# Value, gate and branch projections with the tokens stationary and 512 weight columns moving

## The chip, the cores and the metric

The kernel runs on one core of a Trainium2 chip. The metric is device time in microseconds (us) of one execution, the median of several runs. Engines are named as in the profile: PE is the matrix engine (PEld its weight load), ACT the scalar engine, DVE the vector engine, POOL GpSimd, SP the engine whose queue issues the DMAs.

## What is computed

The program computes a hybrid layer on 256 tokens of width 1024 and then a second block with a mixture of experts. Only the first layer is touched here: one wide projection of the normed tokens `h`, four branches of width 512, and a gated sum of the branches' outputs.

```python
h = rms_norm(x, norm_g)
proj = h @ w_in
(a_u, a_v, a_z, b_q, b_c, ..., d_q, d_k, d_v, d_f, d_z, gates) = jnp.split(proj, points, axis=-1)
# y_a .. y_d: four branches, [tokens, 512] each
ys = jnp.stack([y_a, y_b, y_c, y_d], axis=0)
branch_d = jnp.einsum('nbsw,nwd->bsnd', ys, w_branch)      # 512 -> 1024 for each branch
g = jax.nn.sigmoid(gates.reshape(bsz, s, N_BRANCH, d))      # 4 gates of width 1024
merged = jnp.sum(g * branch_d, axis=2)
return x + merged @ w_out
```

## The kernel before

**Weights and their rounding.** All weights of the first part come in blocks of 128 partitions x 4096 numbers, in the order in which they are used. A block is cut into two halves and four quarters. SP's queue loads a quarter into one of four raw slots, ACT copies it rounded to fp32r into a `w_hi` buffer (L1443), POOL writes the rest of the number into `w_lo` (L2925). There are three buffers for halves (`SPLIT`). ACT may round half h only when the fill that read half h - 3 is complete (`readers`); where in ACT's program that stands is decided by `lead_for`, which puts the rounding ahead of the first evacuation whose fill comes later than that reader.

**Products.** A product of two fp32 matrices is three fp32r matmuls (`matmul3`, L484 to L486): hi x lo, hi x hi, lo x hi. `project_T` keeps 128 weight columns stationary and streams 256 tokens; the result has features on partitions. A block of 512 output columns takes 4 x 8 x 3 = 96 matmuls of 256 columns, and so does a branch block (1024 output columns, 4 contraction chunks). `project_tok` is used for the two value blocks `dv` and `av`: tokens are stationary, but the weight halves are halves of the columns, so that 256 columns move in each matmul too, and both halves of the block are given free by the last fill alone.

**Order of the work.** PE runs a list written out by hand: index block, `bq`, `dq`, `dk`, the values `dv` and `av`, `au`, `az`, `dz`, `bz`, `cb`, `cc`, `cx`, `cz`, with attention pieces in between; then for the branches n in `ORDER` = 0, 3, 2, 1 two gate blocks (fills `g{n}0` to `g{n}3`) and a branch block (`br{n}0` to `br{n}3`). A fill is one PSUM bank of 128 x 512; the projections use banks 0, 1, 2 in turn (`PJ`). ACT evacuates the gate fills with a sigmoid (L1466), DVE multiplies each branch fill with its gate and adds it to `merged` (L2249, L2251), which has features on partitions, as the following product with `w_out` needs it. ACT and DVE run their programs in order too: an instruction that waits holds up all behind it on its engine.

Of the kernel before, what the change touches and what calls it, by code (L numbers as in the profile page):

```python
# [8 lines left out]
D = 1024  # L9
SEQ = 256  # L10
P = 128
# [39 lines left out]
class Fill:  # L51


    def __init__(self, b, n, bank, order):
        self.b, self.n, self.bank, self.order = b, n, bank, order

# [15 lines left out]
def build(nc, A):  # L72
# [3 lines left out]
    with ctx:  # L76
# [91 lines left out]
        PJ, WK = (0, 1, 2), (3, 4, 5, 6, 7)  # L168
        H_BANKS = (7, 1, 6, 3)
# [6 lines left out]
        WO = 26  # L176
        FIN, K0, GF, K1, V0, V1, GF2, WF, Q0, Q1, ZB, GD, WD, WO2 = 28, 29, 30, 31, 32, 33, 34, 35, 36, 37, 38, 40, 42, 44
# [29 lines left out]
        score = [g_(P), g_(SEQ)]  # L207
        lg = {a: [g_(NH * P).rearrange("p (h k) -> p h k", h=NH), g_(NH * SEQ).rearrange("p (h k) -> p h k", h=NH)] for a in "fb"}
# [22 lines left out]
        merged, merged_lo_r = chunked(both(KD * SEQ), KD)  # L231

# [231 lines left out]
        def _(pe):  # L464
# [48 lines left out]
            def project_tok(names, b):  # L513

                fs = [begin(name, PJ, 2 * b + i) for i, name in enumerate(names)]
                readers[2 * b] = fs[1]
                for half in range(2):
                    w = halved(b, half)
                    for t, f in enumerate(fs):
                        for k in range(KD):  # L520
                            last = matmul3(f.bank[:, half * SEQ:(half + 1) * SEQ], [m[:, k, t * P:(t + 1) * P] for m in h1],
                                           [m[:, k * SEQ:(k + 1) * SEQ] for m in w], k == 0, k == KD - 1)
                        if half == 1:
                            end(f, last)
# [185 lines left out]
            for n in ORDER:  # L710
                for half in range(2):
                    project_T([f"g{n}{2 * half + j}" for j in range(2)], GATE[n] + half, h1, SEQ)
                pe.wait_ge(sem(f"y{n}"), 2)
                project_T([f"br{n}{j}" for j in range(4)], WB[n], (y_hi[n], y_lo[n]), SEQ, stride=D, kk=CW)
# [156 lines left out]
            def part_product(f, n, x):  # L871

                w = part_weights(n)
                for k in range(KD):
                    c = slice(k * P, (k + 1) * P)
                    last = matmul3(f.bank[:, n % 2 * SEQ:(n % 2 + 1) * SEQ], [m[:, c] for m in w], [m[:, k, :] for m in x],
                                   k == 0, k == KD - 1)
                last.then_inc(full[f.b] if n % 2 or n == 14 else sem("parts"), 1)

            def first_two(f, n, x_hi, x_lo, hi_at, lo_of, pairs_first):  # L880
# [11 lines left out]
                def lo_products(pair):  # L892
                    pe.wait_ge(sem(lo_of), pair + 1)
                    for j, (w_h, _) in enumerate(both_w):
# [3 lines left out]
                        if pair == 3:  # L898
                            last.then_inc(full[f.b] if j else sem("parts"), 1)
# [1051 lines left out]
        def _(dve):  # L1951
# [286 lines left out]
            for i, n in enumerate(ORDER):  # L2238
                for j in range(4):
                    f = got(f"br{n}{j}")  # L2240
                    dve.wait_ge(sem("gate"), 4 * i + j + 1)
                    m = merged[:, 2 * j:2 * j + 2, :]
# [735 lines left out]
        def _(sp):  # L2978
# [74 lines left out]
            def part_done(n):  # L3053

                if n % 2 == 0 and n < 14:
                    sp.wait_ge(sem("parts"), n // 2 + 1)
# [112 lines left out]

def in_columns(m):  # L3170
# [9 lines left out]
def lay_out(I):  # L3180
# [6 lines left out]
    front += [in_halves(w[n]) for n in "bq dq dk dv av au az dz bz cb cc cx cz".split()]  # L3187
    for n in (0, 3, 2, 1):
        front += parts(w["gates"][:, n * D:(n + 1) * D]) + [in_halves(I["w_branch"][0, n])]
# [51 lines left out]
```

## Time and profile before

| | |
|---|---|
| time, median of 3 runs | 1171.86 us (1171.26 to 1172.09) |
| span of the profiled execution, first to last instruction | 1167.6 us |
| the difference, outside the span | 4.3 us |
| PE busy | 1019.9 us (87%), 8173 matmuls |
| POOL busy | 427.5 us (37%) |
| DVE busy | 506.4 us (43%) |
| chain that ended last, by engine | PE 57%, DMA 27%, DVE 8% |

The span has two parts: up to about 650 us the dense layers, where PE is busy nearly all of the time; after it the experts, where the DMA queues move 428 GB/s and PE waits for weights. Busy time of PE counts an instruction from its start to its modelled end, and these overlap: what a matmul costs in a dense row is the distance from its start to the next one's start, and so the rows below are mostly starts.

### The profile page before, as it was taken

How to read it: one execution, taken by the hardware profiler on the slowest of the kernel's cores; microseconds unless marked ns; L12 is line 12 of the kernel's file. 1: busy time of each engine (PE TensorE's matmuls, PEld its weight loads, DVE VectorE, ACT ScalarE, POOL GpSimd, SP SyncE). 2: the span in 40 equal slices, each digit the busy share in tenths (PEclk: the TensorE clock that was granted, in tenths of full speed). 3: DMA queues.
4: the chain of work that ended last, by engine and by line, in shares of the span. 5: the costliest groups of instructions: out<-in, count | busy, mean ns of one | idle time of the engine just before them, and what ended most of it. 6: DMA issues, size and time to landing. Idle time of an engine off the chain costs nothing.

```text
span 1167.6 us, 20205 instructions
## 1 busy us (share of the span) xinstructions
PE 1019.9 (87%) x8173; PEld 802.9 (69%) x8173; DVE 506.4 (43%) x980; ACT 380.4 (33%) x572; POOL 427.5 (37%) x192
## 2 busy tenths in 40 slices
PE   8999999999999999999999899966767667666685
PEld 6999999999999999797989797423323232332231
DVE  4346965601136887767854543222222222222213
ACT  5554354444447656334343344100000000000002
POOL 6767868888876866143031281000000000000000
PEclk9999999999999999999999899988888888888898
DMA  7644546566656544215220889999999999999995
GB/s 248 219 129 146 178 129 187 175 192 186 183 178 196 165 146 137 59 37 217 93 80 12 326 293 383 388 425 428 429 427 428 429 427 429 428 428 429 428 420 202
DMA packets 43569, 304.75 MB, mean 261 GB/s; under 512 B 5092, under 2 KB 5476, under 8 KB 30952
## 3 DMA queue, kind: packets, MB, share of 16 engines
q1 hardware_dynamic: 43208, 303.21, 69.1%
q8 instruction: 51, 0.84, 0.3%
q10 hardware_dynamic: 288, 0.52, 0.1%
q14 instruction: 22, 0.18, 0.0%
HBM read 302.67 MB, written 1.05 MB: 260 GB/s over the span
## 4 chain that ended last, share of the span: by engine, by line
PE 57%; DMA 27%; DVE 8%; POOL 2%; issue 2%; ACT 2%; SPq 2%; DVEq 0%; ACTq 0%; POOLq 0%
DMA arena<-gate_up 24%; PE bank L484 11%; PE bank L485 11%; PE bank L486 10%; PE bank L1357 6%; PE bank L862 5%; PE bank L1378 3%; POOL rounded L2966 1%; DMA weights<-front 1%; DMA arena<-down 1%; PE bank L826 1%; DVE arena L2091 1%; POOL rounded L2925 1%; SPq L3010 1%; PE bank L1097 1%
## 5 line engine op out<-in xcount | busy, mean ns | idle before, releaser
L2925 POOL TENSOR_TENSOR rounded<-weights,rounded 128x1024 fp32r<-128x1024 f32 x152 | 370.4, 2463 | 156.3 <-ACT rounded L1443 146.9
L484 PE MATMUL bank<-rounded 128*128 128x256 f32 (+2 forms) x776 | 219.2, 282 | 2.2 <-POOL rounded L2925 2.2
L485 PE MATMUL bank<-rounded 128*128 128x256 f32 (+2 forms) x776 | 216.5, 279 | 0.0
L486 PE MATMUL bank<-rounded 128*128 128x256 f32 (+2 forms) x776 | 216.2, 279 | 0.0
L1443 ACT ACTIVATE rounded<-weights 128x1024 fp32r<-128x1024 f32 x146 | 147.4, 1052 | 80.6 <-PE bank L486 47.6
L484 PE MATMUL bank<-rounded,rounded 128*128 128x256 f32 (+3 forms) x552 | 158.3, 287 | 2.1 <-DVEq L2346 0.8
L485 PE MATMUL bank<-rounded,rounded 128*128 128x256 f32 (+3 forms) x552 | 156.2, 283 | 0.0
L486 PE MATMUL bank<-rounded,rounded 128*128 128x256 f32 (+3 forms) x552 | 156.1, 283 | 0.0
L484 PEld LDWEIGHTS bank<-rounded 128*128 128x128 f32 (+1 forms) x776 | 145.6, 188 | 4.3 <-POOL rounded L2925 2.9
L485 PEld LDWEIGHTS bank<-rounded 128*128 128x128 f32 (+1 forms) x776 | 145.5, 187 | 0.7 <-issue 0.6
L486 PEld LDWEIGHTS bank<-rounded 128*128 128x128 f32 (+1 forms) x776 | 145.2, 187 | 0.0
L1357 PE MATMUL bank<-arena 128*32 128x512 f32 x512 | 70.1, 707 | 53.5 <-DMA arena<-gate_up 53.5
L1357 PE MATMUL bank<-weights,arena 128*32 128x512 f32 x512 | 70.2, 710 | 49.9 <-DMA weights<-gate_up 48.9
L484 PEld LDWEIGHTS bank<-rounded,rounded 128*128 128x128 f32 (+1 forms) x552 | 103.2, 187 | 4.4 <-issue 1.7
L485 PEld LDWEIGHTS bank<-rounded,rounded 128*128 128x128 f32 (+1 forms) x552 | 103.3, 187 | 0.1
L486 PEld LDWEIGHTS bank<-rounded,rounded 128*128 128x128 f32 (+1 forms) x552 | 103.1, 187 | 0.1
L2833 DVE TENSOR_TENSOR arena<-arena,bank 128x256 f32<-128x256 f32 x16 | 6.7, 421 | 216.8 <-ACT arena L1902 216.8
L1357 PEld LDWEIGHTS bank<-arena 128*32 128x32 f32 x512 | 17.3, 127 | 100.9 <-DMA arena<-gate_up 53.4
L1357 PEld LDWEIGHTS bank<-weights,arena 128*32 128x32 f32 x512 | 17.9, 128 | 96.7 <-issue 96.7
L1902 ACT ACTIVATE arena<-bank 128x256 f32<-128x256 f32 x16 | 6.1, 384 | 235.7 <-PE bank L1357 235.7
L1390 PE MATMUL bank<-arena 128*128 128x512 f32 x128 | 59.3, 605 | 12.6 <-DVE arena L2838 12.6
L1321 PEld LDWEIGHTS bank<-arena 128*128 128x128 f32 x512 | 59.5, 192 | 8.3 <-issue 8.3
(465 smaller groups left out, 1456.6 us busy)
## 6 DMA issues: line engine op xcount, KB each, us to landing
weights<-front SPq DMA_DIRECT2D x165, 512.0 KB, 4.2
arena<-down SPq DMA_DIRECT2D x31, 2048.0 KB, 22.0
weights<-gate_up SPq DMA_DIRECT2D x28, 2048.0 KB, 34.7
arena<-gate_up SPq DMA_DIRECT2D x28, 2048.0 KB, 33.4
weights<-front SPq DMA_DIRECT2D x4, 2048.0 KB, 8.0
weights<-gate_up SPq DMA_DIRECT2D x8, 768.0 KB, 12.5
arena<-gate_up SPq DMA_DIRECT2D x4, 1536.0 KB, 33.7
weights<-gate_up SPq DMA_DIRECT2D x4, 512.0 KB, 7.3
```

Of the source, the lines that this page charges most:

```text
L484: nc.tensor.matmul(out, a[0], b[1], start=start, stop=False)
L485: nc.tensor.matmul(out, a[0], b[0], start=False, stop=False)
L486: return nc.tensor.matmul(out, a[1], b[0], start=False, stop=stop)
L826: last = nc.tensor.matmul(f.bank[0:SUMS, 0:n], row_of[:, SUMS - 1 - c:2 * SUMS - 1 - c], squares[:, h, 0:n], start=h == 0, stop=h == HEADS ...
L862: last = nc.tensor.matmul(f.bank[:, j * n:(j + 1) * n], w[:, c:c + P], x[:, k, :], start=k == 0, stop=k == KD - 1)
L1097: last = nc.tensor.matmul(o, new_v[l.n][:, i, :], qk[:, l.s + i, :], start=not has_state, stop=True)
L1321: last = nc.tensor.matmul(o, m_tok[:, t, k * P:(k + 1) * P], pick_m[:, t, :], start=t == 0, stop=t == TT - 1)
L1357: last = nc.tensor.matmul(banks[3][j * CAP:(j + 1) * CAP, :], xg[:, k, j * CAP:(j + 1) * CAP], gate_up[u][j][:, k * 2 * FE:(k + 1) * 2 * F ...
L1378: last = nc.tensor.matmul(banks[5 + half][j * CAP:(j + 1) * CAP, :], hid_T[:, i, j * CAP:(j + 1) * CAP], down[u][j // 2][:, c:c + 512], st ...
L1390: nc.tensor.matmul(banks[b][:, :], pick_T[:, i % 2 * P:(i % 2 + 1) * P], yb[:, i // 2 * 512:(i // 2 + 1) * 512], start=True, stop=True).th ...
L1443: nc.scalar.activation(w_hi[h % SPLIT][:, quarter(q)], raw[q % RAW], ACT.Copy).then_inc(sem("w_hi"), 1)
L2925: nc.gpsimd.tensor_tensor(lo, raw[q % RAW], hi.bitcast(f32), ALU.subtract).then_inc(sem("w_lo"), 1)
```

## The change

The two value blocks, the six gate blocks of the first three branches and those three branch blocks now have the tokens stationary (128 tokens of `h`, or of a branch's output) and 512 weight columns moving, so that one matmul does what two did: 48 matmuls of 512 columns in place of 96 of 256, in 11 blocks. Their weights are laid out by contraction rows (`in_rows`): a half holds 4 of the 8 contraction chunks and all 512 columns. Both token tiles are open at once; each is filled by the first half and completed by the second. At the end of the first half PE counts up a semaphore of its own, `weights_read`, and ACT may round over that half from then on. The fills use banks 0 to 3 (`TK`).

The gates and products of the first three branches now have tokens on partitions and are added up in `merged_tok`. The fourth branch stays as it was, with features on partitions. Between its two gate blocks PE turns `merged_tok` round with 16 transposes of 128 x 128 into four banks (`mt0` to `mt3`), ACT copies the four banks into `merged`, and DVE waits for these copies before the fourth branch's first product.

```diff
+            def tok_products(f, w, x, ks, t, first, stop):
+                for i, k in enumerate(ks):
+                    last = matmul3(f.bank[:, :], [m[:, k, t * P:(t + 1) * P] for m in x], [m[:, i * W1:(i + 1) * W1] for m in w],
+                                   first and i == 0, stop and i == len(ks) - 1)
+                return last
+            def project_tok(names, b, pool=PJ):
+                fs, half_k = [], KD // 2
                 for half in range(2):
                     w = halved(b, half)
+                    for t, name in enumerate(names):
+                        if half == 0:
+                            fs.append(begin(name, pool, 2 * b + 1))
+                        last = tok_products(fs[t], w, h1, range(half * half_k, (half + 1) * half_k), t, half == 0, half == 1)
                         if half == 1:
+                            end(fs[t], last)
+                    if half == 0:
+                        last.then_inc(sem("weights_read"), 1)
+                readers[2 * b] = Read(IN_ROWS.index(b) + 1, fs[0].order - 0.5)
+            def branch_tok(n):
+                for half in range(2):
+                    w = halved(WB[n], half)
+                    for t in range(TT):
+                        f = begin(f"br{n}{2 * half + t}", TK, 2 * WB[n] + half)
+                        end(f, tok_products(f, w, (y_hi[n], y_lo[n]), range(CW), t, True, True))
...
-            for n in ORDER:
+            for n in ORDER[:3]:
                 for half in range(2):
-                    project_T([f"g{n}{2 * half + j}" for j in range(2)], GATE[n] + half, h1, SEQ)
+                    project_tok([f"g{n}{2 * half + t}" for t in range(TT)], GATE[n] + half, TK)
                 pe.wait_ge(sem(f"y{n}"), 2)
-                project_T([f"br{n}{j}" for j in range(4)], WB[n], (y_hi[n], y_lo[n]), SEQ, stride=D, kk=CW)
+                branch_tok(n)
+            n = ORDER[3]
+            project_T([f"g{n}{j}" for j in range(2)], GATE[n], h1, SEQ)
+            pe.wait_ge(sem("merged"), 4 * 3)
+            for i in range(4):
+                f = begin(f"mt{i}", TK)
...
+                        last = nc.tensor.transpose(f.bank[:, j * SEQ + t * P:j * SEQ + (t + 1) * P], rows[:, k % 4 * P:(k % 4 + 1) * P], ident)
+                end(f, last)
+            project_T([f"g{n}{2 + j}" for j in range(2)], GATE[n] + 1, h1, SEQ)
+            pe.wait_ge(sem(f"y{n}"), 2)
+            project_T([f"br{n}{j}" for j in range(4)], WB[n], (y_hi[n], y_lo[n]), SEQ, stride=D, kk=CW)
...
                         before = readers[h - SPLIT]
-                        act.wait_ge(full[before.b], before.n + 1)
+                        if isinstance(before, Read):
+                            act.wait_ge(sem("weights_read"), before.value)
+                        else:
+                            act.wait_ge(full[before.b], before.n + 1)
...
+                    if i == 3 and j == 2:
+                        for m in range(4):
+                            f = got(f"mt{m}")
+                            link(nc.scalar.activation(merged[:, 2 * m:2 * m + 2, :], two(f.bank), ACT.Copy))
+                            act.sem_inc(free[f.b], 1)
                     evacuate(f"g{n}{j}", gates[:, 2 * j:2 * j + 2, :], "gate", func=ACT.Sigmoid)
```

The order on PE between the fourth branch's two gate blocks; the names give the bank written, the stationary and the moving operand. Before:

```order
L485 MATMUL bank1<-rounded_20112_2048,rounded_8192_2048 128x256
L486 MATMUL bank1<-rounded_20112_2048,rounded_14336_2048 128x256
L484 MATMUL bank2<-rounded_22160_2048,rounded_4096_2048 128x256 [waits bank2_free,w_lo]
L485 MATMUL bank2<-rounded_20112_2048,rounded_4096_2048 128x256
L486 MATMUL bank2<-rounded_20112_2048,rounded_10240_2048 128x256
```

Now, at the same place:

```order
L497 MATMUL bank1<-rounded_20112_2048,rounded_14336_2048 128x256
L752 MATMUL bank0<-arena 128x128 [waits bank0_free,merged]
L752 MATMUL bank0<-arena 128x128 x3
L752 MATMUL bank1<-arena 128x128 [waits bank1_free]
L752 MATMUL bank1<-arena 128x128 x3
L752 MATMUL bank2<-arena 128x128 [waits bank2_free]
L752 MATMUL bank2<-arena 128x128 x3
L752 MATMUL bank3<-arena 128x128 [waits bank3_free]
L752 MATMUL bank3<-arena 128x128 x3
L495 MATMUL bank2<-rounded_22160_2048,rounded_4096_2048 128x256 [waits bank2_free,w_lo]
```

The fill `g12` goes into bank 2 in both; there the third of the four transposed fills now stands ahead of it.

The order on ACT at that place (L1466 and L1511 are the sigmoid of a gate fill, L1443 and L1488 the rounding of a quarter). Before:

```order
L1466 ACTIVATE arena<-bank1 128x512 [waits bank1_full]
L1443 ACTIVATE rounded_8192_2048<-weights 128x1024 [waits act_chain,slot0_in,bank1_full,merged]
L1443 ACTIVATE rounded_8192_2048<-weights 128x1024 [waits slot1_in]
L1466 ACTIVATE arena<-bank2 128x512 [waits bank2_full]
L1443 ACTIVATE rounded_4096_2048<-weights 128x1024 [waits act_chain,slot2_in,bank2_full,merged]
```

Now:

```order
L1511 ACTIVATE arena<-bank1 128x512 [waits bank1_full]
L1488 ACTIVATE rounded_8192_2048<-weights 128x1024 [waits act_chain,slot0_in,bank1_full,merged]
L1488 ACTIVATE rounded_8192_2048<-weights 128x1024 [waits slot1_in]
L1622 ACTIVATE arena<-bank0 128x512 [waits bank0_full]
L1622 ACTIVATE arena<-bank1 128x512 [waits act_chain,bank1_full]
L1622 ACTIVATE arena<-bank2 128x512 [waits act_chain,bank2_full]
L1622 ACTIVATE arena<-bank3 128x512 [waits act_chain,bank3_full]
L1511 ACTIVATE arena<-bank2 128x512 [waits act_chain,bank2_full]
```

The four copies stand behind the sigmoid of `g11` and behind the rounding of two quarters.

The order on ACT during the block `av`, between the two parts of a softmax's exponentials (L1544, now L1589). Before:

```order
L1544 ACTIVATE arena<-arena 128x256 x3
L1443 ACTIVATE rounded_6144_2048<-weights 128x1024 [waits slot2_in,bank1_full]
L1443 ACTIVATE rounded_6144_2048<-weights 128x1024 [waits slot3_in]
L1443 ACTIVATE rounded_8192_2048<-weights 128x1024 [waits slot0_in,bank1_full]
L1443 ACTIVATE rounded_8192_2048<-weights 128x1024 [waits slot1_in]
```

Now:

```order
L1488 ACTIVATE rounded_6144_2048<-weights 128x1024 [waits slot2_in,weights_read]
L1488 ACTIVATE rounded_6144_2048<-weights 128x1024 [waits slot3_in]
L1589 ACTIVATE arena<-arena 128x256 [waits soft_max]
L1589 ACTIVATE arena<-arena 128x256 x3
L1488 ACTIVATE rounded_8192_2048<-weights 128x1024 [waits slot0_in,bank1_full]
L1488 ACTIVATE rounded_8192_2048<-weights 128x1024 [waits slot1_in]
```

The rounding of the first of the two halves no longer waits for the end of the block (`bank1_full`) but for `weights_read`, and has moved ahead of the second part of the exponentials.

## Rows read from the trace of the kernel before

**Rows 1.** The page, part 4: the chain that ended last, by engine.

```profile
PE 57%; DMA 27%; DVE 8%; POOL 2%; issue 2%; ACT 2%; SPq 2%; DVEq 0%; ACTq 0%; POOLq 0%
```

**Rows 2.** Stretches: us, then busy us of each engine (instructions), clock, DMA share, GB/s.

```profile
204.80:340.50 135.70, 135.70 (x1154) 135.70 (x1153) 37.57 (x39) 60.02 (x68) 114.52 (x48) 1.00 0.62 184
```

**Rows 3.** Timeline of PE (start, us, operation): matmuls of 256 columns.

```profile
89.81 0.28 PE L485 MATMUL bank<-rounded 128*128 128x256 f32 x1
102.73 0.28 PE L485 MATMUL bank<-rounded 128*128 128x256 f32 x1
...
204.83 0.28 PE L485 MATMUL bank<-rounded 128*128 128x256 f32 x1
337.69 0.28 PE L485 MATMUL bank<-rounded,rounded 128*128 128x256 f32 x1
```

**Rows 4.** Timeline of PE: fp32r matmuls of 132 and of 272 columns.

```profile
15.50 0.22 PE L484 MATMUL bank<-rounded 128*128 128x132 f32 x1
15.56 0.28 PE L485 MATMUL bank<-rounded 128*128 128x132 f32 x1
...
384.82 0.29 PE L484 MATMUL bank<-rounded,rounded 128*32 128x272 f32 x1 [0.19 <-DVEq L2315]
387.70 0.29 PE L486 MATMUL bank<-rounded,rounded 128*32 128x272 f32 x1
...
407.58 0.29 PE L485 MATMUL bank<-rounded,rounded 128*128 128x272 f32 x1
431.29 0.29 PE L484 MATMUL bank<-rounded,rounded 128*128 128x272 f32 x1
```

**Rows 5.** Timeline of PE: plain f32 matmuls of 256 columns, and what follows.

```profile
559.65 3.62 PE L862 MATMUL bank<-arena,weights 128*128 128x256 f32 x16
563.10 1.05 PE L993 MATMUL bank<-arena 128*128 128x128 f32 x8
```

**Rows 6.** Timeline of PE: transposes of 128 x 128, and what follows.

```profile
533.68 2.79 PE L849 MATMUL bank<-arena 128*128 128x128 f32 x24
536.40 1.92 PE L956 MATMUL bank<-arena 16*16 16x128 f32 x16
```

**Rows 7.** Timeline of ACT and PE between the fourth branch's two gate blocks.

```profile
317.55 0.28 PE L485 MATMUL bank<-rounded 128*128 128x256 f32 x1
317.98 0.60 ACT L1466 ACTIVATE arena<-bank 128x512 f32<-128x512 f32 x1 [2.48 <-PE bank L486]
318.86 2.01 ACT L1443 ACTIVATE rounded<-weights 128x1024 fp32r<-128x1024 f32 x2 [0.28 <-ACT arena L1466]
```

**Rows 8.** Timeline of PE and ACT around PE's three waits from `av` to `cc`.

```profile
97.72 3.91 ACT L1443 ACTIVATE rounded<-weights 128x1024 fp32r<-128x1024 f32 x4 [6.72 <-PE bank L486]
102.84 0.28 PE L486 MATMUL bank<-rounded 128*128 128x256 f32 x1
104.11 0.38 PE L484 MATMUL bank<-rounded 128*128 128x256 f32 x1 [0.99 <-POOL rounded L2925]
140.91 1.13 PE L637 MATMUL bank<-arena 128*128 128x256 f32 x4 [0.73 <-DVEq L2180]
165.84 0.39 PE L484 MATMUL bank<-rounded 128*128 128x256 f32 x1 [1.19 <-POOL rounded L2925]
```

**Rows 9.** The chain that ended last, in order of time, 60 to 360 us.

```profile
97.79 0.71 DVE arena L2153
...
133.01 0.70 DVE rounded L1985
...
135.22 2.79 DVE rounded L1985
...
160.59 5.21 POOL rounded L2925 x2
```

**Rows 10.** Stretches around two falls of the granted clock; columns as in rows 2.

```profile
653.50:657.70 4.20, 0.10 (x1) 0.00 (x0) 4.10 (x7) 1.64 (x3) 0.50 (x1) 0.86 1.03 400
656.50:663.40 6.90, 5.65 (x26) 5.68 (x27) 5.86 (x9) 4.57 (x7) 5.53 (x3) 0.51 1.03 435
79.50:83.10 3.60, 3.13 (x18) 2.37 (x16) 2.04 (x4) 3.12 (x4) 1.39 (x1) 1.00 0.00 0
83.10:86.50 3.40, 3.40 (x10) 2.72 (x9) 2.07 (x3) 3.37 (x7) 3.40 (x3) 0.50 0.43 108
```

More of the change, by code:

```diff
@@ L55, in __init__ @@
         self.b, self.n, self.bank, self.order = b, n, bank, order
+class Read:
+    def __init__(self, value, order):
+        self.value, self.order = value, order
 class Lane:
@@ L168, in build @@
         PJ, WK = (0, 1, 2), (3, 4, 5, 6, 7)
+        TK = (0, 1, 2, 3)
         H_BANKS = (7, 1, 6, 3)
@@ L176, in build @@
         WO = 26
+        IN_ROWS = [DV, AV] + [GATE[n] + c for n in ORDER[:3] for c in range(2)]
         FIN, K0, GF, K1, V0, V1, GF2, WF, Q0, Q1, ZB, GD, WD, WO2 = 28, 29, 30, 31, 32, 33, 34, 35, 36, 37, 38, 40, 42, 44
@@ L207, in build @@
         score = [g_(P), g_(SEQ)]
+        lg_at = top[0]
         lg = {a: [g_(NH * P).rearrange("p (h k) -> p h k", h=NH), g_(NH * SEQ).rearrange("p (h k) -> p h k", h=NH)] for a in "fb"}
@@ L231, in build @@
         merged, merged_lo_r = chunked(both(KD * SEQ), KD)
+        merged_tok = arena[:, lg_at + 2 * W1:lg_at + 2 * W1 + TT * D].rearrange("p (k t) -> p k t", k=KD)
         top[0] = layer_base
@@ L877, in part_product @@
                                    k == 0, k == KD - 1)
-                last.then_inc(full[f.b] if n % 2 or n == 14 else sem("parts"), 1)
+                last.then_inc(full[f.b] if n % 2 or n == 14 else sem("weights_read"), 1)
             def first_two(f, n, x_hi, x_lo, hi_at, lo_of, pairs_first):
@@ L898, in lo_products @@
                         if pair == 3:
-                            last.then_inc(full[f.b] if j else sem("parts"), 1)
+                            last.then_inc(full[f.b] if j else sem("weights_read"), 1)
                 for pair in range(pairs_first): hi_products(pair)
@@ L2240, in _ @@
                     f = got(f"br{n}{j}")
-                    dve.wait_ge(sem("gate"), 4 * i + j + 1)
-                    m = merged[:, 2 * j:2 * j + 2, :]
+                    dve.wait_ge(sem("gate"), 4 * i + (j if i < 3 else max(j, 2)) + 1)
+                    m = (merged_tok if i < 3 else merged)[:, 2 * j:2 * j + 2, :]
                     g = gates[:, 2 * j:2 * j + 2, :]
@@ L3055, in part_done @@
                 if n % 2 == 0 and n < 14:
-                    sp.wait_ge(sem("parts"), n // 2 + 1)
+                    sp.wait_ge(sem("weights_read"), len(IN_ROWS) + n // 2 + 1)
                 else:
@@ L3167, in in_halves, with in_rows @@
     return m.reshape(-1, P, 2, m.shape[1] // 2).transpose(1, 2, 0, 3).reshape(P, BLOCK)
+def in_rows(m):
+    return m.reshape(2, -1, P, m.shape[1]).transpose(2, 0, 1, 3).reshape(P, BLOCK)
 def in_columns(m):
@@ L3186, in lay_out @@
     front = [in_halves(np.concatenate([w["bc"], w["wi"], w["ki"], w["df"], pad, w["qi"]], 1))]
-    front += [in_halves(w[n]) for n in "bq dq dk dv av au az dz bz cb cc cx cz".split()]
+    front += [(in_rows if n in ("dv", "av") else in_halves)(w[n]) for n in "bq dq dk dv av au az dz bz cb cc cx cz".split()]
     for n in (0, 3, 2, 1):
-        front += parts(w["gates"][:, n * D:(n + 1) * D]) + [in_halves(I["w_branch"][0, n])]
+        gate = w["gates"][:, n * D:(n + 1) * D]
+        front += (parts(gate) if n == 1 else [in_rows(gate[:, :W1]), in_rows(gate[:, W1:])]) + [in_halves(I["w_branch"][0, n])]
     front += parts(I["w_out"][0])
```

12 lines of the change are left out of this document (4 added, 8 removed).

## The prediction, made before the changed kernel was run

> **What bounds the kernel now.** First the chain that ended last: PE holds 57% of it, DVE only 8% [rows 1]. Then the stretch that the change rewrites: from 204.8 to 340.5 us PE does not stop, and the 1154 matmuls that touch it (12 blocks of 96, and two cut by the edges) take 135.7 us; POOL, the next busiest, has 114.5 us to do there [rows 2]. So in the gate and branch blocks a nanosecond saved or added on PE is one on the clock. Around the value blocks it is different: there the chain in order of time leaves PE at 97.79 us, when `av` is complete, and runs over DVE (with few breaks) to 160 us, then over POOL to PE's next wait [rows 9]. What PE saves between these points it may wait out later.
>
> The third view is the pace of PE, start to start. From 204.83 to 337.69 us there are 1128 steps: 117.8 ns for one matmul of 256 columns. From 89.81 to 102.73 us there are 114 steps: 113.3 ns, with the same shapes and the same granted clock [rows 3]. So there are two paces; the change's nine gate and branch blocks ran at the slow one, `av` at the fast one.
>
> **Streaming: 1056 matmuls of 256 columns become 528 of 512.** The streamed columns are the same, 256 columns at 2.4 GHz are 106.7 ns, and what a wider matmul can save is the surcharge: 11.1 ns at the slow pace, 6.7 at the fast one. The question is whether that is paid for each instruction or for each column, and no fp32r matmul of 512 columns is in the trace. Rows nearest to it:
> - 272 columns take 126.1 ns (188 steps from 407.58 to 431.29 us) and 125.2 ns with only 32 stationary columns to load (23 steps from 384.82) [rows 4]. A surcharge of 11.1 ns each would give 113.3 + 11.1 = 124.4; the same price for each column (117.8 / 256 = 0.460 ns) gives 125.2.
> - 132 columns take about 0.06 us [rows 4]. 55 + 11.1 would be 66 ns; 132 x 0.460 is 61.
> - 16 plain f32 matmuls of 256 columns take 3.45 us, 215.6 ns each [rows 5]; at two cycles a column that is 213.3 ns and 2.3 ns of surcharge, though just as many weights are loaded.
>
> The load of the stationary columns therefore isn't the surcharge (32 columns cost what 128 cost), and three lengths of fp32r lie on one price for each column better than on one for each instruction. Bounds for 512 columns: 215.6 ns (rows 5, only the small surcharge left) and 235.6 ns (twice the present matmul, nothing saved). I take 234, near the upper end, since rows 4 are the same data type and rows 5 are not: the price for each column, less part of the 2.3 ns that rows 5 show for each instruction.
> Gates and branches: 432 x (235.6 - 234) = 0.7 us saved. `dv` the same, 48 x 1.6 = 0.1 us if it ran at the slow pace. `av`: 48 x (226.7 - 234), a loss of 0.35 us. Together 0.4 us saved; by the bounds between 0.5 us lost (48 x (235.6 - 226.7) on `av`) and 432 x 20 + 48 x 20 + 48 x 11 = 10.1 us saved.
>
> Of this step the Trainium skill ("TensorE: Matmul & The Clock Gate", section "Back-to-back issue gap") says that a warm matmul of N columns is followed by the next one after N/2.4 + 2.5 ns, which is 215.8 ns for 512 columns and 109.2 for 256. The trace agrees for plain f32 (215.6 ns for 512 cycles, rows 5) and disagrees for fp32r at 256 columns (117.8 and 113.3, rows 3). By the page the sum below would end near 1166.9 us.
>
> **Sixteen transposes and what stands behind them.** A transpose of 128 x 128 costs 113 ns (24 in 2.72 us) [rows 6]: 16 are 1.8 us. The copies by ACT cost more, because of where they stand. As the order shows, ACT first evacuates `g11`, then rounds two quarters, then copies `mt0` to `mt3`; and PE's next fill, `g12`, goes into bank 2, which the third copy sets free. From the trace of that place: ACT starts on `g11` at 317.98 us (0.60 us), starts the rounding at 318.86 and takes 2.01 us, to 320.87 [rows 7]. Three copies of a bank at 0.60 us each, with the 0.28 us between two linked ACT instructions that rows 7 show: 3 x 0.60 + 2 x 0.28 = 2.36, to 323.2, and 0.28 more until PE sees it: 323.5. Before, PE started `g12` at 317.55 [rows 7]. The delay is 6.0 us, of which PE transposes for 1.8, waits 0.7 us or so for bank 1 (`g11` must be out of it before `mt1`) and some 3.3 us for bank 2. ACT and POOL get ahead in this time, but PE was not waiting for them here, so nothing of it comes back; DVE and the fourth branch are all behind `g12`. Bounds: 1.8 us (the transposes alone, all copies hidden) and 6.0 plus a fall of the clock. I take 6.0, since each link is a row and ACT runs in order.
> The clock: after a wait of PE of 4.2 us it was at 1.2 GHz (0.51) for 6.9 us, and after 3.6 us with 18 small matmuls at 1.2 GHz (0.50) for 3.4 us [rows 10]. The new place is like the second. If the clock falls, 3.4 us at half speed cost 1.7 us more. I give that 4 in 10 and leave it out of the middle.
>
> **The read signal.** In `av` ACT rounded nothing from the end of the exponentials until 97.72 us, when the block was complete; that wait was 6.72 us. Four quarters in a row then came late, and PE stood from 102.95 to 104.11 us in `au` [rows 8]: 1.2 us. With `weights_read` the first two quarters are rounded when half of `av` is read, about 5.4 us earlier, and POOL has them done before PE asks. This stop goes. What is late next: PE waits for DVE at 140.91 us already now (0.73) and for POOL at 165.84 (1.19) [rows 8], both ends of the DVE chain that begins with `av`. If that chain stays as it is, all of the 1.2 us is waited out there. But POOL's two quarters leave the stretch in which they hold DVE back (the same DVE instruction takes 0.70 us in one place of the chain and 2.79 in another, rows 9), so that the chain should shorten too. Bounds: nothing, and the three stops together, 3.1 us. I take 1.0. The wait moved ahead of ACT's second part of exponentials delays these by some 5 us; DVE asks for them only after `av`, so it costs nothing; if DVE asked sooner, at most the same 5 us would be at stake.
> In the gate blocks the signal changes nothing: PE never waited for weights there [rows 2].
>
> **Edits that cost nothing.** DVE's products and sums have the same shapes in `merged_tok`. The fourth bank only eases the turns. SP and POOL issue the same transfers and subtractions in the same order.
>
> **The sum.** 1171.9 + 6.0 - 1.0 - 0.4 = 1176.5 us. It is made on one execution with a span of 1167.6 us; the 4.3 us up to the median of the runs lie outside the span and stay. After the gates the chain runs through PE to the experts' loads, which PE's progress releases, so the shift should reach the end whole.
>
> **Rivals.**
> 1. The surcharge is paid for each instruction, and 512 columns cost 215.6 to 224.4 ns (213.3 and 2.3 or 11.1). For: the fast pace exceeds 106.7 ns by the same 16 cycles in every step, as a fixed cost would. Against: rows 4. With 221 ns: 432 x 14.6 + 48 x 14.6 + 48 x 5.7 = 7.3 us saved, 1171.9 + 6.0 - 1.0 - 7.3 = 1169.6 us, faster; with 215.6 ns 1166.8, with 224.4 ns 1171.5. It decides in favour of the change from about 221 ns down. The skill's gap rule is this rival's lower end.
> 2. The price is by the column, but the wide matmuls run at the fast pace, 0.443 ns a column or 226 ns with a little off. For: `av`, tokens stationary, ran at it. Against: `project_T` blocks ran at both paces, so the form didn't decide it. 432 x 9.6 + 48 x 9.6 = 4.6 us saved: 1172.3 us, no difference.
> 3. The change doesn't do what it says at the read signal: PE's stop in `au` goes, and all of it returns at 140.91 and 165.84 us. Then the forecast ends at 1177.5 us; a fall of the clock as well gives 1179.2.
>
> **Chances and range.** Forecast with rival 3 (1175 to 1179): 0.53. Rival 1: 0.30. Rival 2: 0.17. A measurement of this kernel can tell 0.2%, 2.3 us, from no change: faster is below 1169.5, slower above 1174.2. Faster: two thirds of rival 1, 0.20. Same: the rest of rival 1, most of rival 2 and a little of the forecast, 0.26. Slower: 0.54. The range must reach into rival 1, down to 217 to 218 ns for 512 columns, 1168.0; at the top it takes in the fall of the clock, 1179.0.
>
> **What would show it.** Right: starts of the 512-column matmuls 233 to 236 ns apart in the gate blocks; PE stopped for 3 us or more ahead of `g12`, released by ACT's copy line, 6 us from the last matmul of `g11` to the first of `g12`; no stop in `au`, a longer one at the logits of `b`. Wrong: starts 216 to 222 ns apart (rival 1), or 226 (rival 2); ACT's copies done before the rounding, so that PE goes on after 2 us.

## The result, and the profile after

| | before | after |
|---|---|---|
| time, median of 19 runs each | 1171.41 us (1167.12 to 1175.79) | 1175.0 us (1169.97 to 1178.52) |
| ratio, 95% interval | | 1.0027 (1.0015 to 1.0038) |
| span of the profiled execution | 1167.6 us | 1173.3 us |
| PE busy, matmuls | 1019.9 us, 8173 | 1026.5 us, 7661 |

The changed kernel is slower by 0.27%, 3.6 us where 4.6 were forecast. For each of its runs the span is known too: it is 1.7 to 1.8 us below the time, and 1.7 to 2.0 in 43 of the 45 runs of the kernel before that list it. By that the profiled execution of before, with its span of 1167.6 us, was one of about 1169.3 us, 2 us better than the median, and the 4.3 us that were put outside the span were in part that difference. One run of e3 (below), 1678.6 us at a mean granted clock of 0.554, is left out of its figures.

Page, part 4, the chain that ended last, by engine (answers [rows 1]):

```profile
PE 60%; DMA 26%; DVE 5%; ACT 2%; POOL 2%; issue 2%; SPq 2%; ACTq 0%; DVEq 0%; POOLq 0%
```

Three points of the chain, some 35 us, have passed from DVE to PE. From 97.8 to 129 us the chain of before ran over DVE; now DVE is done sooner there and waits for PE, as its row at 125.27 us shows below.

**The wide matmuls.** Timeline of PE, the second 512-column matmul of the gates and the last of the third branch (answers [rows 3]), and the stretch between them, with the columns of [rows 2]:

```profile
204.77 0.40 PE L496 MATMUL bank<-rounded 128*128 128x512 f32 x1
...
305.10 0.40 PE L497 MATMUL bank<-rounded,rounded 128*128 128x512 f32 x1
```

```profile
204.80:305.10 100.30, 100.30 (x432) 80.81 (x430) 35.52 (x29) 43.70 (x49) 87.12 (x37) 1.00 0.62 184
```

430 steps in 100.33 us are 233.3 ns each; 234 was taken. 432 of them are 0.97 us less than 864 at 117.8. In `av`, which had run at 113.3 ns, the 48 wide ones cost 0.32 us more (233.3 against 226.7).

**The place of the transposes.** Timeline of PE and ACT between the fourth branch's two gate blocks (answers [rows 7]; L1511 is the sigmoid, L1488 the rounding, L1622 the copies):

```profile
316.52 0.28 PE L497 MATMUL bank<-rounded 128*128 128x256 f32 x1
316.64 0.60 PE L752 MATMUL bank<-arena 128*128 128x128 f32 x4
316.84 0.60 ACT L1511 ACTIVATE arena<-bank 128x512 f32<-128x512 f32 x1 [2.77 <-PE bank L497]
317.54 1.53 PE L752 MATMUL bank<-arena 128*128 128x128 f32 x12 [0.29 <-ACTq L1512]
317.71 2.00 ACT L1488 ACTIVATE rounded<-weights 128x1024 fp32r<-128x1024 f32 x2 [0.27 <-ACT arena L1511]
319.62 2.72 ACT L1622 ACTIVATE arena<-bank 128x512 f32<-128x512 f32 x4
321.81 0.55 PE L495 MATMUL bank<-rounded 128*128 128x256 f32 x1 [2.75 <-ACTq L1623]
322.16 0.41 PE L496 MATMUL bank<-rounded 128*128 128x256 f32 x1
```

From the last matmul of `g11` to the first of `g12` PE needs 321.81 - 316.52 = 5.29 us, where one step of 0.12 us stood: 5.2 us lost, 6.0 forecast. The reader should see the order on ACT: sigmoid, two roundings, and only then the four copies, the third of which ends the 2.75 us wait. And the matmuls that follow stand 0.21 us apart instead of 0.118: the clock fell to 0.50, 1.2 GHz. The same columns as above, for the stretch of the stop and the one behind it:

```profile
316.60:321.80 5.20, 2.18 (x18) 1.71 (x17) 0.00 (x0) 4.33 (x7) 4.29 (x3) 0.95 0.64 197
321.80:324.60 2.80, 2.79 (x13) 2.80 (x14) 0.00 (x0) 0.54 (x1) 1.71 (x1) 0.50 0.79 199
```

**The read signal.** ACT and PE from `av` to `cc` (answers [rows 8]):

```profile
92.16 2.01 ACT L1488 ACTIVATE rounded<-weights 128x1024 fp32r<-128x1024 f32 x2 [5.17 <-PE bank L497]
97.76 2.01 ACT L1488 ACTIVATE rounded<-weights 128x1024 fp32r<-128x1024 f32 x2 [1.62 <-PE bank L497]
...
139.67 1.13 PE L665 MATMUL bank<-arena 128*128 128x256 f32 x4 [0.49 <-DVEq L2230]
164.84 0.38 PE L495 MATMUL bank<-rounded 128*128 128x256 f32 x1 [1.43 <-POOL rounded L2975]
```

Two quarters are rounded at 92.16 us instead of behind 97.72, PE's stop in `au` is gone, and the later waits are 0.49 and 1.43 us (0.73 and 1.19 before). PE starts the logits at 139.67 instead of 140.91: 1.2 us are kept. The next two rows, one of before and one of after, show why the chain of DVE shortened with it: the same four instructions, first beside twelve subtractions of POOL in a row, then for the most part in a pause of POOL (115.44 to 118.03 us). The third row, of after, is DVE's next one: it waits for PE.

```profile
118.67 10.20 DVE L2091 SCALAR_TENSOR_TENSOR arena<-arena 128x256 f32<-128x256 f32 x4
```

```profile
116.64 4.07 DVE L2141 SCALAR_TENSOR_TENSOR arena<-arena 128x256 f32<-128x256 f32 x4
125.27 0.70 DVE L2239 TENSOR_TENSOR bank<-bank,arena 128x512 f32<-128x512 f32 x1 [4.55 <-PE bank L712]
```

The Trainium skill ("SBUF — State Buffer", section "SBUF: two separate sides") says that VectorE and GpSimd share a port pair that one of them holds for a whole instruction. The trace agrees: 10.20 against 4.07 us, of which the three instructions in POOL's pause took 0.48 us each and the fourth, beside POOL, 2.52.

**What the clock did elsewhere.** Summed over stretches of 1 us up to 700 us (busy time of PE times one minus the granted clock), the falls of the clock cost 6.2 us in three places before and 9.7 us in six places after. One of these is the fall behind the stop (1.4 us); two more (1.7 us each, at 457 and 468 us) lie in code that the change doesn't touch. Between 698 and 785 us, where the experts' weights are awaited, the lag of the changed kernel shrinks from 8.6 to 6.3 us. That is no waiting out of the lag: e1 (below), level with the kernel before at 698 us, gains 1.8 us in the same stretch, and the second profile of before (e10) loses 0.5. SP issues twelve transfers of experts' weights there in 7.1 us in the changed kernel and 7.9 in e1, and in 8.7 in either profile of before; why is not shown.

### The profile page after: what moved, and what is told of

The parts are those of the page before. It is cut to its first block, busy times and chain, and to the rows that moved or that the text cites. A ratio compares the mean times of both kernels' runs of the same rounds, so it can differ in the third digit from the quotient of the medians.

```text
span 1173.3 us, 19188 instructions
## 1 busy us (share of the span) xinstructions
PE 1026.5 (87%) x7661; PEld 785.7 (67%) x7661; DVE 502.9 (43%) x980; ACT 382.3 (33%) x576; POOL 425.1 (36%) x192
## 4 chain that ended last, share of the span: by engine, by line
PE 60%; DMA 26%; DVE 5%; ACT 2%; POOL 2%; issue 2%; SPq 2%; ACTq 0%; DVEq 0%; POOLq 0%
DMA arena<-gate_up 24%; PE bank L495 12%; PE bank L497 11%; PE bank L496 11%; PE bank L1399 6%; PE bank L904 5%; PE bank L1420 3%; DMA weights<-front 1%; POOL rounded L3016 1%; PE bank L868 1%; POOL rounded L2975 1%; DMA arena<-down 1%; SPq L3060 1%; PE bank L1139 1%; PE bank L1118 1%
## 5 line engine op out<-in xcount | busy, mean ns | idle before, releaser
L495 PE MATMUL bank<-rounded 128*128 128x256 f32 (+3 forms) x648 | 199.1, 307 | 4.2 <-ACTq L1623 2.7
L497 PE MATMUL bank<-rounded 128*128 128x256 f32 (+3 forms) x648 | 196.2, 303 | 0.0
L496 PE MATMUL bank<-rounded 128*128 128x256 f32 (+3 forms) x648 | 196.2, 303 | 0.0
L1488 ACT ACTIVATE rounded<-weights 128x1024 fp32r<-128x1024 f32 x146 | 147.1, 1052 | 98.5 <-PE bank L497 78.3
L495 PE MATMUL bank<-rounded,rounded 128*128 128x256 f32 (+4 forms) x504 | 151.4, 300 | 2.7 <-POOL rounded L3016 1.0
L497 PE MATMUL bank<-rounded,rounded 128*128 128x256 f32 (+4 forms) x504 | 149.1, 296 | 0.0
L496 PE MATMUL bank<-rounded,rounded 128*128 128x256 f32 (+4 forms) x504 | 149.0, 296 | 0.0
L495 PEld LDWEIGHTS bank<-rounded 128*128 128x128 f32 (+1 forms) x648 | 122.0, 188 | 12.1 <-POOL rounded L2975 5.1
L496 PEld LDWEIGHTS bank<-rounded 128*128 128x128 f32 (+1 forms) x648 | 121.9, 188 | 6.1 <-issue 0.2
L497 PEld LDWEIGHTS bank<-rounded 128*128 128x128 f32 (+1 forms) x648 | 122.0, 188 | 5.8
L495 PEld LDWEIGHTS bank<-rounded,rounded 128*128 128x128 f32 (+1 forms) x504 | 95.0, 188 | 7.2 <-issue 1.8
L496 PEld LDWEIGHTS bank<-rounded,rounded 128*128 128x128 f32 (+1 forms) x504 | 95.0, 189 | 2.3
L497 PEld LDWEIGHTS bank<-rounded,rounded 128*128 128x128 f32 (+1 forms) x504 | 95.0, 188 | 2.3
L1399 PEld LDWEIGHTS bank<-arena 128*32 128x32 f32 x512 | 17.7, 129 | 97.8 <-DMA arena<-gate_up 51.8
```

The costliest lines, as they stand in the source:

```text
L495: nc.tensor.matmul(out, a[0], b[1], start=start, stop=False)
L496: nc.tensor.matmul(out, a[0], b[0], start=False, stop=False)
L497: return nc.tensor.matmul(out, a[1], b[0], start=False, stop=stop)
L1399: last = nc.tensor.matmul(banks[3][j * CAP:(j + 1) * CAP, :], xg[:, k, j * CAP:(j + 1) * CAP], gate_up[u][j][:, k * 2 * FE:(k + 1) * 2 * F ...
L1488: nc.scalar.activation(w_hi[h % SPLIT][:, quarter(q)], raw[q % RAW], ACT.Copy).then_inc(sem("w_hi"), 1)
```

## The experiments

**Take the stop away.** First another four banks for the transposed fills, then DVE as well in place of ACT for the copies:

```diff
-                f = begin(f"mt{i}", TK)
+                f = begin(f"mt{i}", (4, 5, 6, 7))
```

```diff
-                        for m in range(4):
-                            f = got(f"mt{m}")
-                            link(nc.scalar.activation(merged[:, 2 * m:2 * m + 2, :], two(f.bank), ACT.Copy))
-                            act.sem_inc(free[f.b], 1)
...
+                if i == 3:
+                    for m in range(4):
+                        evacuate(f"mt{m}", merged[:, 2 * m:2 * m + 2, :])
```

> The changed kernel, but the four transposed fills go into banks 4 to 7 instead of 0 to 3, so that the fill g12 no longer needs the bank that ACT's third copy sets free; ACT's copies stay where they are. Theory 'bank wait': in the changed kernel PE went from the last matmul of g11 (316.52 us) to the first of g12 (321.81) in 5.3 us and then ran 12 matmuls at the low clock (1.2 us lost). Here that step takes 1.9 to 2.2 us (16 transposes at 113 ns), the clock stays at 1.00, and 4.3 to 4.6 us come back: about 1170.5 us, ratio to the kernel before 0.9985 to 1.0000. Rival 'ACT is the limit': the copies still stand ahead of the sigmoid of g12 and of the next rounding, PE stops later at a bank of g13 or of the branch, and the time stays within 1 us of the changed kernel's 1175.0. Rival 'the transposes lower the clock': the step is short but the half clock comes all the same, 1171.7 us.

> As e1_far_banks, and the four copies are made by DVE, which was busy 0.00 us between 316.5 and 322 us, instead of ACT. Theory 'bank wait': with the banks out of the way the copies are hidden anyway, so this lies within 0.5 us of e1_far_banks in the trace up to the end of the fourth branch. Rival 'ACT is the limit': at least 1 us faster than e1_far_banks there, since 2.7 us of copies leave ACT's program.

Measured: 1168.04 us, ratio to before 0.9971 (0.9960 to 0.9982), and 1168.01 us, 0.9969 (0.9955 to 0.9983). Timeline of PE and ACT at the place in e1, and the clock of the two stretches behind it:

```profile
314.76 1.91 PE L752 MATMUL bank<-arena 128*128 128x128 f32 x16
314.96 0.60 ACT L1511 ACTIVATE arena<-bank 128x512 f32<-128x512 f32 x1 [2.77 <-PE bank L497]
315.83 2.01 ACT L1488 ACTIVATE rounded<-weights 128x1024 fp32r<-128x1024 f32 x2 [0.27 <-ACT arena L1511]
316.43 0.36 PE L495 MATMUL bank<-rounded 128*128 128x256 f32 x1
317.74 2.73 ACT L1622 ACTIVATE arena<-bank 128x512 f32<-128x512 f32 x4
```

```profile
316.40:319.20 2.80, 2.80 (x27) 2.80 (x26) 0.00 (x0) 2.56 (x5) 2.23 (x1) 1.00 0.72 200
319.20:321.60 2.40, 2.40 (x23) 2.40 (x23) 0.00 (x0) 1.16 (x2) 2.40 (x2) 1.00 0.50 125
```

ACT copies at the same point of its program as in the changed kernel, but PE is back on `g12` 1.67 us after the first transpose, and the clock stays at 1.00. So the bank was the wait, the clock did not fall where PE did not stop, and ACT was not the limit: in e2, without the copies, the trace is that of e1 within 0.1 us up to 480 us. The gain was larger than expected, 7 us against 4.6. Of it 3.5 us are the stop, 1.4 to 3.1 the clock behind it, and 0.85 us a surprise: in e1 and e2 the matmuls from 316.6 to 338 us ran at 113.3 ns instead of 117.8 (191 steps); in e7, with the same banks, they ran at 117.8. This version beats both kernels. The terms account for 0.3 us of the 3.4 under the kernel before (1.7 for the transposes, less 1.0 at the read signal and 1.0 for the wide matmuls of gates and branches); the 1.8 us at the experts are the largest other piece that the traces show.

**One half of the change each.** e3 is the kernel before with `dv` and `av` changed and nothing else (`IN_ROWS = [DV, AV]`); e6 is e1 with these two blocks as before (`IN_ROWS` without them).

> The kernel before with the two value blocks dv and av alone changed (512 columns moving, halves by rows, read signal); gates and branches as before, no transposes. Theory: PE reaches its wait for POOL at cc (before: first matmul after it at 165.84) about 1.2 us earlier, as in the changed kernel; the blocks cx and cz decide how much of it is left at the first gate: if they run at 117.8 ns as in the changed kernel 0.2 us, if at 113.3 as in the kernel before 1.1 us; the gates and branches then take as long as before. Time 1170.3 to 1171.4, ratio 0.9990 to 1.0000. Rival 'the loss is in the value blocks': ratio 1.002 or more.

> The other half of e3: gates and branches as in e1_far_banks (512 columns moving, read signal, transposed fills in banks 4 to 7), the two value blocks as in the kernel before. Theory: up to the first gate it is the kernel before, with its stop in au; then the nine blocks give back 1.0 us (432 times 235.6 - 233.3) and the transposes cost 1.8: about 1 us over the kernel before, ratio 0.9995 to 1.0015. Rival 'the gates carry the gain': e1_far_banks was 3.5 us under the kernel before and e3_values_only 2.6, so that this part would bring 0.9 us of its own: ratio 0.9985 to 0.9995.

Measured: e3 1168.4 us in the median and 1169.5 in the mean of eleven runs, 0.9981 (0.9967 to 0.9996); e6 1169.57 us, 0.9988 (0.9973 to 1.0003). The product, 0.9969, is what e1 and e2 have: within these intervals the halves add up. e3 gained 2.2 us, more than the 0.2 to 1.1 expected, though its interval reaches down to 0.5; its trace is 1.2 us ahead of before at 141 us, as in the changed kernel. e6 doesn't separate its two theories. Its trace agrees with the first up to `g12` (317.75 us against 317.55, with 0.4 us gained by chance in `dv`); after that the fast pace as in e1 gives 0.85 us back, which neither theory had.

**Take the read signal away**, in all eight blocks:

```diff
-                readers[2 * b] = Read(IN_ROWS.index(b) + 1, fs[0].order - 0.5)
+                readers[2 * b] = fs[1]
```

> The changed kernel without the read signal: ACT waits for the end of the block again before it rounds over a first half, in all eight blocks. Theory 'the chain shortens': PE's stop of some 1.2 us in au returns (near 103 us), the DVE chain behind it stretches again, PE starts the logits of b near 141 us instead of 139.67, and the first gate comes about 1.2 us later than in the changed kernel: ratio to the kernel before 1.003 to 1.004. Rival 'absorbed': the stop in au returns, but the waits at the logits of b and at cc shrink by as much, and from 166 us on the trace is that of the changed kernel: ratio 1.0027.

Measured: 1184.04 us, 1.0102 (1.0082 to 1.0121): 9 us above the changed kernel, not 1.2. Waits of PE in the gates and branches, two of them in the timeline, and ACT ahead of the first:

```profile
PE bank L495 <- POOL rounded L2975: 7.6, 6, 1.3
```

```profile
218.14 3.90 ACT L1488 ACTIVATE rounded<-weights 128x1024 fp32r<-128x1024 f32 x4 [0.25 <-ACT arena L1511]
...
224.06 0.50 PE L495 MATMUL bank<-rounded 128*128 128x512 f32 x1 [1.21 <-POOL rounded L2975]
236.74 0.50 PE L495 MATMUL bank<-rounded,rounded 128*128 128x512 f32 x1 [1.20 <-POOL rounded L2975]
```

The stop in `au` returns (0.78 us), and the wait at the logits grows to 3.00 us, so "absorbed" is wrong. But most of the loss lies where nothing was expected: six stops of 1.2 to 1.3 us, ahead of the second half of the second gate block and of the branch block, for each of the three branches. In the kernel before, the first half of a gate block was free when the first of two fills was complete, in the middle of the block. With halves by contraction rows no fill completes before the end; the half that takes that buffer (three halves later) is rounded late, four quarters come due at once, and POOL needs some 2.4 us for each. The signal gives back what the new layout of the weights takes away.

**The falls of the clock: place or chance?** Both kernels once more.

> The changed kernel once more, for a second profile. Theory 'the falls of the clock come by chance except where PE stops': the fall behind g12 (322 to 325 us) comes again, with the 2.7 us wait for ACT ahead of it; the falls at 82 and 457 to 472 us need not come at the same places. Rival 'every fall belongs to its place': all six falls at the same places as in the first profile.

> The kernel before once more, for a second profile of it. Theory 'falls by chance': the fall at 83 to 87 us need not come again, nor the fast pace in av, cx and cz; the span differs from 1167.6 us by the count of falls times 1.7 us and some tenths of pace. Rival 'every fall and every pace belongs to its place': the same falls, the same blocks at 113.3 ns.

The same two stretches in the first and the second profile of the kernel before (the clock is the number before the DMA share):

```profile
83.00:87.00 4.00, 4.00 (x14) 3.21 (x14) 2.29 (x5) 3.97 (x10) 4.00 (x3) 0.57 0.45 126
452.00:456.00 4.00, 4.00 (x35) 4.00 (x36) 3.30 (x8) 3.62 (x7) 2.32 (x1) 1.00 0.56 156
```

```profile
83.00:87.00 4.00, 4.00 (x29) 3.79 (x29) 3.50 (x5) 3.97 (x10) 4.00 (x3) 1.00 0.44 125
452.00:456.00 4.00, 4.00 (x24) 4.00 (x23) 2.98 (x7) 3.79 (x6) 1.37 (x1) 0.57 0.77 222
```

One fall is gone and another has come, with the same program (0.57 over a stretch of 4 us is a fall to 0.50 for most of it). `cx` and `cz`, at 113.3 ns in the first profile, ran at 117.8 in the second. In the changed kernel's second profile the fall behind `g12` came again, and cost 3.1 us; the one at 82 us did not. Over all ten profiles of the layer, the fall behind `g12` is there in the three that have the stop and in none of the seven that don't. That one belongs to its place. So do two that the change doesn't touch, near 11 and at 656 to 677 us, which all ten profiles have; the others come and go, at 1.6 to 1.7 us each. The mean granted clock of all runs is in line with this: the span times one minus that clock is 67.2 us on average in the 19 runs of the changed kernel, 65.9 in 45 of the kernel before, and 64.5 and 65.0 in the 12 each of e1 and e2.

**What does a wide matmul cost?** First in the kernel: e1 with each matmul of 512 columns cut into two of 256.

> e1_far_banks with each 512-column matmul cut into two of 256 with the same stationary block (weights loaded twice): the layout without the wide matmul. Theory 'price per column': the gate and branch blocks of the first three branches run at 117.8 ns a piece, 1.0 us longer than in e1_far_banks from the first gate to the last matmul of the third branch (100.5 us there), or, where they start at the fast pace, at 113.3, which is 2.9 us shorter. Rival 'a price for each instruction': more than 4 us longer in every case.

Timeline of PE, a matmul of the first gate block and the last one before the transposes:

```profile
205.64 0.28 PE L495 MATMUL bank<-rounded 128*128 128x256 f32 x1
...
313.65 0.28 PE L497 MATMUL bank<-rounded 128*128 128x256 f32 x1
```

953 steps in 108.0 us: 113.3 ns. A pair costs 226.7 ns where the wide one costs 233.3, so that the narrow form was 2.9 us shorter over 432 pairs. (One run: 1167.65 us.)

Then by itself, in programs of trains of 48 matmuls, each after a stop of another length. They compute no output.

> Not the layer: a program of matmuls alone (no output is computed, zeros are written), to measure the disputed price by itself. Trains of 48 fp32r matmuls of one width, stationary blocks of 128 columns, each train after a stop of PE of another length. Widths 64 to 512, then 14 trains each of 256 and 512 in turn, then 272 and 384; two trains with only 32 stationary columns, two in plain f32. Theory 'price per column': start to start 0.456 ns a column for all widths of 256 and more, 512 always near 233.3 ns, 384 near 175, and 256 now at 117.8, now at 113.3 ns, decided at a train's start. Rival 'a price for each instruction': 512 near 224, 384 near 171. Rival 'the wide matmuls have a fast pace too': some of the 14 trains of 512 run near 226.7 ns.

> Again matmuls alone (no output is computed, zeros are written), 256 and 512 columns in the patterns of the kernel, since in e5 a matmul of 512 columns took 227 ns and not the 233.3 of the changed kernel. Patterns: alternating operands; the same, added up in one bank; the kernel's three products (hi x lo, hi x hi, lo x hi) written anew and added up; with the roles of the two tensors swapped; one stationary block and one moving block all the time. Theory 'the order of operands sets it': the three products give 233.3 ns for 512 columns and 113.3 or 117.8 for 256 with every other engine idle. Rival 'adding up in PSUM sets it': both added-up patterns give 233.3. Rival 'the other engines' (their reads of the same memory): every pattern stays at 227 here, and at 120 for 256 columns.

> Matmuls alone a third time (zeros are written), now with the buffers of the kernel itself: tokens (h, hi and lo) and weights (the three buffers w_hi and w_lo) at their places, in the order of tok_products with 512 and with 256 columns and in that of project_T. Of the five rounds of nine trains the third and fourth run beside transfers into the raw slots, the fifth beside POOL's subtractions. Theory 'the places of the operands': 512 columns take 233.3 ns in every round, and 256 take 117.8 or 113.3. Rival 'the transfers': 227 in the first two rounds, 233.3 in the third and fourth. Rival 'the compute engines': 227 but in the fifth. If all rounds show 227 and 120, none of the three is the reason, and it stays open.

> Matmuls alone a last time (zeros are written): the weights stay at their place, the tokens are moved through memory, to offsets of 0 to 1680 columns (modulo 2048) from the weights; 1680 is where the kernel's h lies, 0 is the layout of e5 and e9; both come twice. For each offset one train of 512 columns and one of 256 with the tokens stationary, two of 256 with the weights stationary. Theory 'the distance of the operands sets the pace': 0 gives 227 and 120 ns, 1680 gives 233.3 and 113.3 or 117.8, in both places of the list, and the offsets between group with the one or the other. Rival 'it was something else in the layout' (the spacing of the hi and lo buffers, the blocks' strides): every offset gives the same.

In e5 none of the theories held whole: inside a train 256 columns took 119.9 ns, 320 took 146.7, 384 took 173.3 and 512 took 227, which is N / 2.4 and 13.3 ns for each instruction (448 took 202.7, 2.7 ns more than that, and 272 took 125.2 to 126.7). The 227 ns are those of the last theory, but all 15 trains had them, and 256 stayed at 120. With 32 stationary columns 256 took 117.8 and 512 took 231.7. e9 has the kernel's order and adds up in PSUM, and stays at 227 and 120. e11 has the kernel's buffers at their places: 512 columns take 233.3 ns in all 15 trains, beside transfers and POOL or not. e12 moves the tokens only. Timeline of PE, trains of 48; the second number is the length of the train. At offset (in columns from the weights, modulo 2048) 1680, then 0, 16 and 64, each time 512 columns and then 256 with the tokens stationary:

```profile
45.08 11.46 PE L491 MATMUL bank<-rounded,rounded 128*128 128x512 f32 x48 [0.51 <-ACT arena L504]
57.10 5.73 PE L491 MATMUL bank<-rounded,rounded 128*128 128x256 f32 x48 [0.56 <-ACT arena L504]
...
76.61 11.22 PE L491 MATMUL bank<-rounded,rounded 128*128 128x512 f32 x48 [0.69 <-ACT arena L504]
88.55 6.02 PE L491 MATMUL bank<-rounded,rounded 128*128 128x256 f32 x48 [0.73 <-ACT arena L504]
...
108.22 11.46 PE L491 MATMUL bank<-rounded,rounded 128*128 128x512 f32 x48 [0.44 <-ACT arena L504]
120.16 5.73 PE L491 MATMUL bank<-rounded,rounded 128*128 128x256 f32 x48 [0.48 <-ACT arena L504]
...
139.45 11.21 PE L491 MATMUL bank<-rounded,rounded 128*128 128x512 f32 x48 [0.61 <-ACT arena L504]
151.33 6.02 PE L491 MATMUL bank<-rounded,rounded 128*128 128x256 f32 x48 [0.66 <-ACT arena L504]
```

11.46 us are 233.3 ns inside the train, 11.2 are 227; 5.73 are 113.4, 6.02 are 120. The offsets 1680 (twice) and 16 give the first pair, the offsets 0 (twice), 64, 128, 256, 512, 1024, 1536 and 1664, all multiples of 64 columns, the second; both offsets of the first group are 16 above a multiple of 64, and no other was tried. So the place of the tokens in memory sets the price, and it decides which form is cheaper: 233.3 against 2 x 113.4, or 227 against 2 x 120. Whether their distance from the weights counts or their own address is not shown, since the weights stayed at a multiple of 2048. At the kernel's offset one more thing counts, the form: with tokens stationary 11 of 15 trains of 256 ran at 113.4 ns in e11, with weights stationary 2 of 15. With weights stationary in e12 256 took 117.8 ns at 1680 and 16, 120 at the other offsets. What the memory does there is not shown.

One row of the kernel before belongs to this, the third of the group of 132 columns whose first two [rows 4] show:

```profile
15.67 0.28 PE L486 MATMUL bank<-rounded 128*128 128x132 f32 x1
```

The first step of each such group is 60 to 63 ns, the second 110; in a longer row, from 20.1 to 22.5 us, these matmuls stand 110 to 114 ns apart.

## Why the prediction was right, and where not

- **What bounds the kernel.** Held: PE didn't stop in the gates, and what PE lost at `g12` was lost to the stages behind it, as e1 shows from the other side.
- **Streaming, -0.4 us.** The taken price was 234 ns, the measured one 233.3, and the blocks gained 0.8 us together (0.97 in gates and branches, 0.1 in `dv`, less 0.32 in `av`). The reason given for it, a price for each column, is no law: e5 shows the price for each instruction of rival 1, at 227 instead of 215.6 to 224.4 ns, at offsets that the kernel doesn't have. The prediction's rows could not tell that, since their tokens lay at the kernel's own places. One of its three lengths also says less than was taken from it: the 0.06 us of 132 columns are the first step of a group of three (60 to 63 ns each time), and the next step in the same group is 0.11 (15.56 to 15.67 us), as in longer rows of them. Rival 2's fast pace for wide matmuls came in none of 15 trains of e11 and in none of the kernel's profiles; the argument against it, that the form doesn't decide the pace, was too strong, since it shifts the odds.
- **The stop ahead of `g12`, +6.0 us.** The mechanism was the predicted one, link by link; it measured 5.2, and the wait in it 2.75 us where 3 or more were named as the sign. The copies follow one another in 0.71 us, where 0.60 and 0.28 had been added (0.35 us for three), and the rounding ended 0.3 us earlier after the last matmul of `g11`. 16 transposes take 1.67 us (e1) and not 1.8.
- **The clock, left out at 4 in 10.** This is the term that was mis-sized: the fall came in all three profiles with the stop and cost 1.4 to 3.1 us. It belonged in the middle of the sum, and the 1.7 us named for it fit two of the three; in the second profile of the changed kernel (e8) the fall lasted twice as long.
- **The read signal, -1.0 us.** Right in size (PE 1.2 us ahead at the logits, 1.0 behind its wait at `cc`) and in mechanism: POOL's work moved ahead of DVE's, and DVE's chain shortened. Rival 3 fell. The sign that PE's wait at the logits would be longer did not come: it was 0.49 us, not 0.73, and only the one at `cc` grew, by 0.24. Wrong was the sentence that the signal changes nothing in the gate blocks. It was tested against the kernel before, where a fill did what the signal does now; without it the new layout costs 9 us (e4).
- **The sum.** With the clock's 1.4 us it would have been 5.2 + 1.4 - 1.0 - 1.0 = 4.6 us (the first 1.0 is the lead behind `cc`, with the value blocks' 0.1 and 0.32 in it, the second the gates and branches); 3.6 were measured, with an interval of 1.8 to 4.5. That this is again the 4.6 of the forecast is luck: a stop taken 0.8 us too long and a saving taken 0.6 too small made up for the clock that was left out. The pace of blocks that nothing touched accounts for tenths in either direction (`cx` and `cz` 0.85 us), single falls of the clock for 1.7. "The shift should reach the end whole" held up to 698 us (PE 5.4 us late from 338 to 440 us, 8.6 at 698 with two falls more); behind that the profile of after gains 2.3 us, and e1, which had no lag, 1.8, so that it was not the lag that was waited out there. What it was stays open.

## What to carry to other kernels

When a step is inserted on PE, ask which bank the next fill takes and where the instruction that frees it stands in its engine's order: the 16 transposes cost 1.7 us with free banks and 5.2 us with a bank freed by the third copy behind two roundings, and a stop of that kind costs the clock behind it too. When the layout of a shared buffer changes, ask what now tells its reader that a part is free; a signal that looks like an addition may be the replacement of one that the layout removed. And a price for each column or each instruction should be measured at the operands' own addresses before a change is built on it.

## What was not expected of the hardware

- An fp32r matmul of 256 columns took 113.3, 117.8 or 120 ns and one of 512 took 227 or 233.3, at the full clock, with the same instructions; moving the tokens by 16 columns (e12, offsets 0 and 16) changes the pair. Where 113.3 and 117.8 are both open, the pace is set at the start of a row of matmuls and stays until PE's next break or next other work, in every row of 256 up to 345 us of all ten profiles. The Trainium skill ("TensorE: Matmul & The Clock Gate", section "Back-to-back issue gap") gives N/2.4 + 2.5 ns for the isolated gap, and for a stream of loads and matmuls about 131 ns at 512 columns. The formula fits plain f32 here only (215.8 ns for 512 cycles in e5), and fp32r has 13.3 ns in place of 2.5 where the offset is a multiple of 64 columns; no run here shows the 131.
- The falls of the clock differ from execution to execution of one program: three in either profile of the kernel before, of which only two lie at the same place; six and four in the changed kernel. A difference of 1.7 us between single runs needs no other cause.
